# Products without a reader in TensorE's pauses around a router

## The reference

```python
t = rms_norm(x, g)                                  # 512 x 1024
g_sel = argmax(t @ w_group + b_group)               # 1 of 4 groups
e_logit = (t @ w_er + b_er)[g_sel]                  # 8 experts of that group
top_v, top_i = top_k(e_logit, 2)
gate = softmax(top_v) * p_g
for each expert e of 32, on its tokens (padded in blocks):
    y_e = (silu(x_e @ w_gate[e]) * (x_e @ w_up[e])) @ w_down[e]
x = x + sum of gate * y_e
```

## Time and profile before

| | |
|---|---|
| median of 3 runs | 1636.0 us (1635.77 to 1645.68) |
| the profiled execution | 1641.42 us, its span 1639.6 us |
| TensorE busy | 1403.5 us, 86% of the span |
| VectorE, ScalarE, GpSimd busy | 32%, 15%, 12% |
| mean granted clock of TensorE | 0.936 |
| DMA, mean over the span | 292 GB/s; about 405 to 415 in the middle of the expert stages |

### The profile page before, as it was taken

How to read it: one execution, slowest core, us unless ns; L and a number is a source line. 1 busy time by engine, 2 the same in 40 slices (tenths; PEclk the granted TensorE clock), 3 DMA queues, 4 the chain that set the end, 5 groups by cost and what they waited for, 6 DMA issues and landing times. The chain is left out here.

```text
span 1639.6 us, 18872 instructions
## 1 busy us (share of the span) xinstructions
PE 1403.5 (86%) x7021; PEld 665.2 (41%) x7021; DVE 527.6 (32%) x1240; ACT 243.9 (15%) x522; POOL 191.4 (12%) x362
## 2 busy tenths in 40 slices
PE   7999999979978887887889978897988888878886
PEld 3545674554423332332334556455333333323332
DVE  6999983241111110111041169224110101111114
ACT  3211111111100000000020047121100000000002
POOL 5200000011111111111000000001211111111100
PEclk9999999969999999999899989997998999999999
DMA  8215345469999999999995100546999999999996
GB/s 252 105 65 88 49 160 214 152 241 368 395 405 409 406 415 408 412 402 405 417 346 193 52 1 2 205 175 253 368 404 408 410 407 406 405 403 411 406 417 255
DMA packets 74021, 479.22 MB, mean 292 GB/s; under 512 B 17204, under 2 KB 24116, under 8 KB 49392
## 3 DMA queue, kind: packets, MB, share of 16 engines
q1 hardware_dynamic: 61392, 454.36, 70.9%
q0 software_dynamic: 11152, 19.27, 3.5%
q10 hardware_dynamic: 1424, 4.89, 0.8%
HBM read 468.01 MB, written 26.74 MB: 302 GB/s over the span
## 5 line engine op out<-in xcount | busy, mean ns | idle before, releaser
L680 PE MATMUL psum<-ring,work 128*64 128x512 f32 x992 | 486.7, 648 | 118.3 <-DMA ring<-in_moe_w_up 116.5
L681 PE MATMUL psum<-ring,work 128*64 128x512 f32 x992 | 487.1, 649 | 0.0
L680 PEld LDWEIGHTS psum<-ring,work 128*64 128x64 f32 x992 | 143.3, 149 | 434.7 <-issue 344.4
L693 PE MATMUL psum<-ring,work 128*64 128x512 f32 x992 | 226.5, 598 | 28.2 <-DVE work L864 28.2
L861 DVE TENSOR_TENSOR work<-work,psum 64x512 f32<-64x512 f32 x64 | 44.1, 690 | 593.2 <-ACT work L818 593.1
L818 ACT ACTIVATE work<-psum 64x512 f32<-64x512 f32 x64 | 37.8, 590 | 826.6 <-PE psum L681 826.6
L681 PEld LDWEIGHTS psum<-ring,work 128*64 128x64 f32 x992 | 143.4, 150 | 1.9
L693 PEld LDWEIGHTS psum<-ring,work 128*64 128x64 f32 x992 | 67.1, 137 | 142.6 <-issue 126.0
L867 DVE COPY work<-psum 128x512 f32<-128x512 f32 x60 | 41.5, 691 | 231.1 <-PE psum L693 231.1
L1767 PE MATMUL psum<-ring,hT 128*128 128x512 f32 x256 | 113.7, 601 | 0.0
L1057 POOL COPY ints<-ints 64x1 uint32 (+1 forms) x64 | 11.4, 178 | 527.4 <-PE psum L672 490.0
(11 more groups left out here) (378 smaller groups left out, 1395.4 us busy)
## 6 DMA issues: line engine op xcount, KB each, us to landing
ring<-in_moe_w_gate SPq DMA_DIRECT2D x62, 2048.0 KB, 17.7
ring<-in_moe_w_up SPq DMA_DIRECT2D x62, 2048.0 KB, 22.9
ring<-in_moe_w_down SPq DMA_DIRECT2D x62, 2048.0 KB, 23.3
ring<-in_hyb_w_in SPq DMA_DIRECT2D x5, 2048.0 KB, 8.9
work<-y_dram SPq DMA_DIRECT2D x8, 1024.0 KB, 9.4
ring<-in_swa_w_qkv SPq DMA_DIRECT2D x3, 2048.0 KB, 17.2
x_sb<-in_x SPq DMA_DIRECT2D x8, 512.0 KB, 6.1
y_dram<-x_sb SPq DMA_DIRECT2D x1, 4096.0 KB, 18.5
```

Source lines behind the costliest of these rows:

```text
L680: nc.tensor.matmul(bank[2 + b][0:BLK, :], XT[b][:, c, :], g[:, c, :], start=c == 0, stop=c == KC - 1)
L681: i = nc.tensor.matmul(bank[2 + b][BLK:P, :], XT[b][:, c, :], u[:, c, :], start=c == 0, stop=c == KC - 1)
L693: i = nc.tensor.matmul(bank[6 + b][BLK * hf:BLK * (hf + 1), :], HTE[b][:, c, :], d[:, c, hf * HALF:(hf + 1) * HALF], start=c == 0, stop=c ...
```

## The change

A helper, `pe_keep_busy`, issues f32 products of the identity with up to 512 columns of a table of constants into a PSUM bank, and nothing reads them. The bank is always 6. It is called at six places of TensorE's program, once per layer each; a number is the width of a product in columns:

- ahead of the logits of tile 2: 512, 512, behind a new wait for the sixth addition to x;
- ahead of the logits of tile 3, behind the transposes of that tile: 256;
- behind the logits of tile 3, ahead of the counts: seven of 512;
- behind the counts, ahead of the lists: 512, 512, 256;
- behind the lists, ahead of the transposes of expert 0's rows: 512, 512, 512, 256;
- behind those transposes, ahead of expert 0's gate and up: 512.

```diff
--- before.py
+++ after.py
@@ -412,6 +412,11 @@
         ov = [{k: sem(f"ov{l}_{k}") for k in ("w", "i", "xg", "xt", "xe", "gu", "a", "h", "ht", "he", "dn", "y", "st")}
               for l in range(2)]
 
+        def pe_keep_busy(b, *widths):
+
+            for w in widths:
+                nc.tensor.matmul(bank[b][:, 0:w], ident, CT[:, P:P + w], start=True, stop=True)
+
         def pe_logits(pe, l, t):
 
             pe.wait_ge(n_ea.s, NT * (2 * l + 1) + t + 1)
@@ -431,6 +436,7 @@
             pe.wait_ge(g_zero.s, 1)
             nc.tensor.matmul(bank[1][:, 0:NE], cst("before"), rt("S"), start=True, stop=True).then_inc(g_C.s, 1)
             nc.tensor.matmul(bank[3][:, 0:NE], ONES[:, :], rt("S"), start=True, stop=True).then_inc(g_C.s, 1)
+            pe_keep_busy(6, 512, 512, 256)
 
             pe.wait_ge(g_exr.s, 4 * l + 3)
             pe.wait_ge(g_L.s, l + 1)
@@ -771,8 +777,10 @@
                                              start=False, stop=True)
                 i.then_inc(mg_mm.s, 1)
 
+            pe_keep_busy(6, 512, 512, 512, 256)
             pe.wait_ge(xg_ld[0], 16 * (NE // 2) * l + 16)
             pe_x(0, e_xt)
+            pe_keep_busy(6, 512)
             step(0, 0, first=True)
             pe_overflow_lists(pe, l)
             step(1, 1)
@@ -1723,9 +1731,13 @@
                     pe_norm_tile(pe, 2 * l + 1, t - 1)
                 if n and t > 1:
                     pe_logits(pe, l, t - 2)
+            pe.wait_ge(o_ev.s, 8 * l + 6)
+            pe_keep_busy(6, 512, 512)
             pe_logits(pe, l, NT - 2)
             pe_norm_tile(pe, 2 * l + 1, NT - 1)
+            pe_keep_busy(6, 256)
             pe_logits(pe, l, NT - 1)
+            pe_keep_busy(6, *([512] * 7))
 
         def pe_mixer0(pe):
             pe.wait_ge(id_in, 32)
```

## The result

The changed kernel is faster by 0.8%: the ratio to the kernel before is 0.9921, 95% interval 0.9906 to 0.9936, or 13 us of the 1642.3 us that 20 runs of the kernel before now have as their median (10.5 to 15.4); its own median over 20 runs is 1629.9 us. The forecast was 12 us (0.7%), and within 1% the likeliest case.

A forecast was written before the change was run, and what follows sets the result against it. The prediction took TensorE's small products on the chain of waits, slowed to half clock after pauses, as the bound; savings of 6.6 us (layer 0) and 5.3 (layer 1), together 11.9, take 1636.0 to 1624 us, range 1618 to 1632.

The forecast's parts named there:

- The mechanism: Router to expert 0: fillers hold TensorE at full clock, expert 4's gate load comes about 6.6 us earlier, savings reach the end.
- Logits and transposes: Router tiles 2 and 3, layer 0: logits save 1.73 us each, transposes 0.91; layer 1: 0.10, 1.73 and 0.9.
- The counts: Behind the logits of tile 3: nothing saved, because VectorE's scan covers the first count.
- It fits with about 0.2 to spare: Ahead of the transposes of x: 3.5 fillers, 3.0 us, fit a pause grown from 1.64 to some 3.2 us.
- The filler behind those transposes: Ahead of expert 0: 0.86 us in a pause of 0.68, taken as 0.1 over; with the transposes, net -0.05.
- Expert 0: Gate and up at full clock: 1.52 us saved in layer 0, 1.79 in layer 1.
- The weak place: List products behind the third filler group: clock may fall, one chance in three per layer, costing 1.3 to 1.5 us.
- The new wait: Ahead of the first fillers: the wait for the sixth addition to x is long over, as earlier products needed that bank.
- transposes that do not hold the clock: Between first fillers and logits of tile 3: clock falls, 3.2 us lost per layer, 1630 us; chance 0.09.
- a gain swallowed by the weight stream: Expert stage: weight loads set their own pace, so an earlier expert 0 only waits longer, 1636 us; chance 0.06.
- more than the sum: Whole run: gain of 17 us and up, 1619 or less, needing 4.5 us no row shows; chance 0.05.
- The slower rival: All filler groups: fillers at half clock overrun their pauses by 14.7 us per layer, 1665 us; chance 0.04.

The follow-up runs named there:

- cut kernel: Changed kernel with the group ahead of the transposes of x cut by 512 columns and the one behind them to 256; ratio 0.9910 to the kernel before.
- longer: Changed kernel with one more filler of 512 columns in every group; ratio 0.9972 to the kernel before.
- wide: The cut kernel with fillers also in pauses of both layers' mixers; ratio 0.9896 to the kernel before.
- half-length kernel: Changed kernel with each group at about half: 1, 0, 3.5, 1.25, 1.75 and a half fillers; ratio 0.9954 to the kernel before.

## Why the prediction held, and where its steps did not

- **The mechanism** held: the clock at 1.00 through the stage, the small steps near their full-clock times, the load of expert 4 moved with TensorE, and the end with the load. The DMA engines were idle between 344.2 and 349.2 us, but not over the whole stage, as "not full before that" has it: the earlier trace rows have a share of 0.91 to 1.02 at 323 to 328.5 and at 352.6. The gain came through all the same.
- **Logits and transposes**: 1.73 was forecast for the logits of tile 2 in layer 0 and of tile 3 in both layers, 0.91 for the transposes. From start to start they gave 1.63, 1.64 and 0.82; the logits of tile 2 in layer 1 gave 0.01 in place of 0.10. Sixteen logit records behind a wait take 1.95 us, not the 1.87 of those in a row of products; the price came from a row that had not waited.
- **The counts** gave nothing, as said: from VectorE's first operation behind the logits to the counts it is 6.03 us before (335.08 to 341.11) and 6.04 after (327.38 to 333.42).
- **"It fits with about 0.2 to spare"**, of the 3.5 fillers ahead of the transposes of x, is the step that failed. The group ended last in both layers: 0.67 us were saved from list to transposes in layer 0, 0.32 in layer 1, in place of 0.79. In layer 0 the terms were too small: the target lists took 1.76 us from start to start (337.53 to 339.29) and not 1.6, the fillers 3.20 (339.29 to 342.49) and not 3.0. In layer 1 the pause before was also 0.34 us shorter than in layer 0 (6.20 from list to transposes against 6.55), and I had measured layer 0's alone. The prediction named a step behind a filler that starts without any pause as a sign that it was wrong; at this group, and at the next, which it had priced as held up, the sign came true. The cut kernel gives both layers' loss back.
- **The filler behind those transposes** cost 0.26 us of the path in place of the 0.05 of the sum.
- **Expert 0**: 1.47 and 1.74 saved, against 1.52 and 1.79.
- **The weak place** was misplaced. I gave one chance in three that the clock falls between the counts and expert 0; in twelve stages with full-length dense fillers or transposes (this kernel twice, the kernels with transposes, cut, longer and wide) it never did. It fell one step later, over the transposes and lists behind expert 0's gate and up, in six of those twelve. I had read 1.00 there in the earlier trace rows and taken one execution's row for a rule; the second profile of the kernel before has the fall in the same place. In the fourteen other stages that is the only one, so the change may move a fall there; that is not shown.
- **The new wait** for the sixth addition was over, but not for the reason given: the projection's last tile waits for the fifth. The sixth had come because the logits of tile 1, which stand ahead of the wait, need the rows that it completes.
- **The rivals**: transposes that do not hold the clock, and a gain swallowed by the weight stream, are out by the runs above, and more than the sum (17 us and up) by the interval. The slower rival is real with other fillers, and priced right to about 1 us per layer.

So the sum of 11.9 had 1.7 us too much against the first profile before, and that profile's stage in layer 1 was 2.8 us short of the second's: two errors that nearly cancel. That the sum came within a microsecond of the mean of both (11.6) is luck to that extent. Open: which share of the falls behind expert 0 ends up in the run, and why the half-length kernel is faster than its stages.

## What to carry to other kernels

Where small products of one engine stand on the path after a pause, look at the granted clock before looking for anything else; filling the pause with dense work that nobody reads is worth the half-clock share of the steps behind it, and no more. Size each filler by the shortest of its pauses over all layers and end it a little short, because a filler that ends last is paid in full, and one that starts at half clock takes twice as long; at half the length the clock fell in all four stages. Judge it in the stage, over several profiles: single executions of one kernel lay as far apart (12 and 18 us) as the change moved the median.

## What was not expected of the hardware

- TensorE busy for 15.00 of 15 us by the trace, nearly all of it products of 36 columns, and the granted clock 0.50 all that time; in the same places products of 512 columns, of the same total length at full clock, held 1.00.
- 128x128 f32 transposes as fillers held the clock at 1.00 as well as products did, over a stretch of 35 us whose last 7 are expert 0's own products.
- The clock fell at different steps in two executions of one kernel: the same logits took 1.97 and 3.60 us.
